# The first expert's rows turned by matmuls: known rows gathered early, the last two tiles put in with token-by-slot matrices

## The reference

```python
hp = hp + _mix_out(attn_p, bp * conv_p, ...)          # output projection
tok = concat([_rmsnorm(hp), _rmsnorm(hs)])            # 1032 tokens x 1024
g_sel = argmax(tok @ w_rg + b_rg)                     # one of 4 groups
le_sel = (tok @ w_re + b_re)[group g_sel]             # 8 logits
top_v, top_i = lax.top_k(le_sel, 2)
gates = softmax(top_v) * p_group[g_sel]
# for each expert e, over the rows that chose it:
hid = silu(xb @ w_gate[e]) * (xb @ w_up[e])           # 1024 -> 512
y = hid @ w_down[e]                                   # 512 -> 1024
# out = residual + gates[0] * y0 + gates[1] * y1, then a final norm
```

## Time and profile before

| | us |
|---|---|
| median of 3 runs | 1163.91 |
| lowest to highest run | 1163.84 to 1164.36 |
| the profiled execution's own time | 1163.65 |
| its span | 1161.8 |
| TensorE busy in the span | 1129.5 |
| VectorE busy | 826.4 |
| ScalarE busy | 640.8 |

### The profile page before, as it was taken

The page is one execution under the profiler, slowest core; times in us unless marked ns, Lnnn a source line. Parts: engine busy times, 40 slices in busy tenths (PEclk is TensorE's granted clock), DMA queues, the critical chain, the costliest instruction groups (busy, mean ns, idle before and its releaser), DMA issues.

```text
span 1161.8 us, 17492 instructions
## 1 busy us (share of the span) xinstructions
PE 1129.5 (97%) x7026; PEld 884.7 (76%) x7026; DVE 826.4 (71%) x1172; ACT 640.8 (55%) x796; POOL 106.3 (9%) x130
## 2 busy tenths in 40 slices
PE   7999999999999999999999999999999999999994
PEld 6999999999857768886677777777777777777761
DVE  5314434322387658887898898898898898889886
ACT  7221230211078732334577777777777777778744
POOL 1002110012000000000011100101100100112110
PEclk9999999999999999998999999999999999999998
DMA  8116474333050051114999999999999999999777
GB/s 257 55 44 194 126 240 160 119 109 110 5 179 21 26 221 73 74 73 163 372 400 399 384 391 382 388 399 381 382 391 385 381 393 383 383 388 376 308 266 292
DMA packets 77941, 292.54 MB, mean 252 GB/s; under 512 B 9689, under 2 KB 34393, under 8 KB 52962
## 3 DMA queue, kind: packets, MB, share of 16 engines
q1 hardware_dynamic: 66178, 259.78, 59.0%
q0 software_dynamic: 11680, 31.62, 8.3%
HBM read 270.09 MB, written 33.77 MB: 262 GB/s over the span
## 4 chain that ended last, share of the span: by engine, by line
PE 92%; DVE 4%; DMA 2%; ACT 1%; issue 1%; SPq 0%; DVEq 0%; POOLq 0%; ACTq 0%
PE psum L1190 10%; PE psum L1188 10%; PE psum L1189 10%; PE psum L854 8%; PE psum L856 8%; PE psum L855 8%; PE psum L1217 5%; PE psum L1219 5%; PE psum L1218 5%; PE psum L989 3%; PE psum L991 2%; PE psum L990 2%; PE psum L1177 2%; PE psum L939 2%; PE psum L955 1%; PE psum L933 1%
## 5 line engine op out<-in xcount | busy, mean ns | idle before, releaser
L854 PE MATMUL psum<-h_hi,w_hi 128*128 128x344 f32 (+2 forms) x576 | 185.8, 323 | 3.1 <-DVE h_lo L1684 3.0
L856 PE MATMUL psum<-h_hi,w_lo 128*128 128x344 f32 (+2 forms) x576 | 184.0, 319 | 0.0
L855 PE MATMUL psum<-h_lo,w_hi 128*128 128x344 f32 (+2 forms) x576 | 184.0, 319 | 0.0
L2115 DVE TENSOR_TENSOR w_down_lo<-w_down,w_down_hi 128x2048 fp32r<-128x2048 f32 x62 | 139.7, 2288 | 40.6 <-ACT w_down_hi L1507 40.6
L2115 DVE TENSOR_TENSOR w_gate_lo<-w_gate,w_gate_hi 128x2048 fp32r<-128x2048 f32 x64 | 144.2, 2288 | 20.7 <-ACT w_gate_hi L1507 19.4
L2115 DVE TENSOR_TENSOR w_up_lo<-w_up,w_up_hi 128x2048 fp32r<-128x2048 f32 x64 | 143.7, 2286 | 2.4
L1507 ACT CAST w_gate_hi<-w_gate 128x2048 fp32r<-128x2048 f32 x64 | 119.6, 1911 | 9.1 <-DMA w_gate<-in_w_gate 8.8
L1507 ACT CAST w_up_hi<-w_up 128x2048 fp32r<-128x2048 f32 x64 | 119.9, 1917 | 2.2 <-DMA w_up<-in_w_up 2.1
L1507 ACT CAST w_down_hi<-w_down 128x2048 fp32r<-128x2048 f32 x62 | 115.7, 1906 | 3.9 <-DMA w_down<-in_w_down 3.9
L854 PEld LDWEIGHTS psum<-h_hi,w_hi 128*128 128x128 f32 x576 | 108.2, 188 | 5.5 <-DVE h_lo L1684 3.9
L856 PEld LDWEIGHTS psum<-h_hi,w_lo 128*128 128x128 f32 x576 | 108.2, 188 | 0.0
(11 more groups left out here) (287 smaller groups left out, 1911.6 us busy)
## 6 DMA issues: line engine op xcount, KB each, us to landing
w_gate<-in_w_gate SPq DMA_DIRECT2D x64, 1024.0 KB, 16.2
w_up<-in_w_up SPq DMA_DIRECT2D x64, 1024.0 KB, 17.3
w_down<-in_w_down SPq DMA_DIRECT2D x64, 1024.0 KB, 15.5
w_raw<-in_w_in SPq DMA_DIRECT2D x24, 512.0 KB, 4.0
y_tile<-y_rows SPq DMA_DIRECT2D x16, 512.0 KB, 10.4
kv<-in_cache_k POOLq DMA_DIRECT2D x24, 256.0 KB, 4.6
kv<-in_cache_v POOLq DMA_DIRECT2D x24, 256.0 KB, 4.6
x_tile<-in_x_prompt SPq DMA_DIRECT2D x8, 512.0 KB, 5.5
```

The costliest lines, as they stand in the source:

```text
L854: mm(ps, wh[:, k, :], h_hi[:, k, cols], start=(k == 0), stop=False)
L855: mm(ps, wh[:, k, :], h_lo[:, k, cols], start=False, stop=False)
L856: ins = mm(ps, wl[:, k, :], h_hi[:, k, cols], start=False, stop=(k == KD - 1))
L2115: vec.tensor_tensor(dst[:, part, :], src[:, part, :], hi[:, part, :].bitcast(F32), ALU.subtract).then_inc(split, 1)
```

## The change

The table in HBM is laid out so that the seven tiles finished first come first (`token_row`: 776 rows, `KNOWN`), and the last two tiles last. After `place` of p = 6, which TensorE now does one step earlier, VectorE makes the first expert's indices from the table so far (`rows_known`), and GpSimd gathers those rows into a cleared buffer `xg_first`; slots whose tokens are in the last two tiles are still empty in that table, are dropped by the bounds check and stay zero.

TensorE puts these rows into PSUM with eight matmuls against the identity (`first_rows_fetched`), and adds the last two tiles straight from `h2` in SBUF: eight matmuls each of `h2` with a 0/1 matrix `chosen` of token by slot (`first_rows_chosen`). VectorE builds `chosen` from the rank in PSUM with `unchosen`, which moves tokens that did not choose the expert out of range (`choose_rows`).

The `keep_clock(3)`, `keep_clock(5)` and `keep_clock_narrow(12)` matmuls are gone. The first expert's products are written apart: for gate, then up, hi x hi and lo x hi (`first_upper`), then the count for further blocks, then both hi x lo series (`first_lower`). VectorE does `lower_rows` right behind the last tile's count, before the tables, and the splits of gate and up before `count_all`. `fetch_issued` is gone, so SyncE's loads are no longer held back by it; the second expert's down load waits for `xT_ready`, since its buffer is `xg_first`'s.

```diff
+KNOWN = NTOK - 2 * P
+def token_row(t):
+    return P * (t - 2) if t >= 2 else KNOWN + P * t
...
@@ SyncE
-            load_gate(first, 1, 1, (0,))
+            load_gate(first, 1, 1)
             store_h2(NT - 1)
-            sp.wait_ge(fetch_issued, 1)
-            load_gate(first, 1, 1, (1,))
+            load_down(first, 0, 0)
             load_up(first, 1, 1)
-            load_down(first, 0, 0)
+            store_residual(NT - 1)
+            sp.wait_ge(first.xT_ready, 2)
             load_down(first, 1, 1)
-            store_residual(NT - 1)
@@ TensorE
                     if n == 3:
                         route_pair(p - 1, 0)
                         route_pair(p - 1, 1)
+                        if p == NT - 1:
+                            place(p - 2)
...
-            keep_clock(3, bank(0), 512)
+            def first_rows_fetched():
+                pe.wait_ge(lg_used, NT)
+                pe.wait_ge(first.rows_in, 16)
+                for k in range(KD):
+                    mm(bank(4 + k // 4)[:, (k % 4) * SLOTS:(k % 4 + 1) * SLOTS], xg_first[:, k * P:(k + 1) * P],
+                       ident[0:SLOTS, 0:SLOTS], start=(k % 4 == 0), stop=True, skip_group_check=True)
+            def first_rows_chosen(p):
+                w = rows(turn[p])
+                pe.wait_ge(h2_ready, p + 1)
+                pe.wait_ge(chosen_ready, p - (NT - 2) + 1)
+                for k in range(KD):
+                    ins = mm(bank(4 + k // 4)[:, (k % 4) * SLOTS:(k % 4 + 1) * SLOTS],
+                             h2[p % 2][0:w, k * P:(k + 1) * P], chosen[p % 2][0:w, :], start=False, stop=True,
+                             skip_group_check=True)
+                    if p == NT - 1 and k % 4 == 3:
+                        ins.then_inc(first.xT_ready, 1)
+            first_rows_fetched()
+            first_rows_chosen(NT - 2)
             rank(NT - 1)
+            first_rows_chosen(NT - 1)
             place(NT - 1)
...
-            keep_clock(5, bank(0), 512)
-            keep_clock_narrow(12)
-            pe.wait_ge(routed, 1)
-            pe.wait_ge(first.rows_in, 16)
-            turn_rows(first)
+            first_upper(wg_hi, 0, first.gate_hi)
+            first_upper(wu_hi, 1, first.up_hi)
             count_all()
+            first_lower(wg_lo[0], 0, first.gate_split, first.gate_done)
+            first_lower(wu_lo[0], 1, first.up_split, first.up_done)
@@ ScalarE
+            act.wait_ge(h2_out[1], 16 * 4)
+            upper_rows(first, 0)
             act.wait_ge(gd_ready, 1)
             nc.scalar.activation(r_g, r_g, ACT.Exp)
             nc.scalar.activation(r_v, r_v, ACT.Exp).then_inc(gexp_ready, 1)
-            upper_rows(first, 0)
@@ VectorE
+            def choose_rows(p, e):
+                w = rows(turn[p])
+                step(vec.tensor_scalar(unchosen[p % 2][0:w, :], r_hot[p % 2][0:w, e:e + 1], DROP, -DROP,
+                                       ALU.mult, ALU.add))
+                if p == NT - 1:
+                    router_rows(p)
+                dve.wait_ge(ranked, p + 1)
+                vec.scalar_tensor_tensor(out=chosen[p % 2][0:w, :], in0=ramp[0:w, 0:SLOTS],
+                                         scalar=unchosen[p % 2][0:w, :],
+                                         in1=bank(6)[0:w, NE + e:NE + e + 1].broadcast_to([w, SLOTS]),
+                                         op0=ALU.add, op1=ALU.is_equal).then_inc(chosen_ready, 1)
...
+            rows_known(order[0])
             choose_first(NT - 2)
...
             recip_ffn(NT - 1)
+            choose_rows(NT - 2, order[0])
             slots_of(NT - 2)
             choose_first(NT - 1)
             choose_second(NT - 1)
-            router_rows(NT - 1)
+            choose_rows(NT - 1, order[0])
             slots_of(NT - 1)
+            count_tile(NT - 1)
...
+            lower_rows(first, 0)
             dve.wait_ge(hot_used, 2 * NT)
...
-            dve.wait_ge(fetch_issued, 1)
             lower_gate(first, 0, 0)
+            lower_up(first, 0, 0)
             count_all()
-            lower_rows(first, 0)
-            lower_up(first, 0, 0)
             finish_gates()
@@ GpSimd
+            pool.wait_ge(a_ready, NT - 1)
+            gp.memset(xg_first, 0.0).then_inc(rows_clear, 1)
+            pool.wait_ge(h2_out[0], 16 * 4)
+            pool.wait_ge(h2_out[1], 16 * 3)
+            pool.wait_ge(rows_clear, 1)
+            pool.wait_ge(routed, 1)
+            fetch(first, gi_s, xg_first, KNOWN)
             pool.wait_ge(h2_out[0], 16 * 5)
             pool.wait_ge(h2_out[1], 16 * 4)
-            pool.wait_ge(routed, 1)
-            fetch(first, gidx[:, order[0]:order[0] + 1])
-            gp.memset(stat[0:1, 82:83], 0.0).then_inc(fetch_issued, 1)
-            pool.wait_ge(y_cleared, 16 * NT)
+            pool.wait_ge(routed, 2)
```

More of the change, by code:

```diff
@@ L65, in constants @@
     c = np.arange(P)[None, :]
-    tok = 128 * np.arange(NT)[None, :] + p + 1
+    tok = np.array([token_row(t) for t in range(NT)])[None, :] + p + 1
     const = np.concatenate([
@@ L239, in program @@
         r_tab2 = rt_end("r_tab2", [NE])
+        chosen = [rt_end(f"chosen{s}", [SLOTS]) for s in range(2)]
+        unchosen = [rt_end(f"unchosen{s}", [1]) for s in range(2)]
         over = Pack(WEI + 3 * 16384, WEI + 4 * 16384)
@@ L382, in program @@
         all_sent = sem("all_sent")
-        fetch_issued = sem("fetch_issued")
+        rows_clear = sem("rows_clear")
         table_warm = sem("table_warm")
@@ L704, in store_h2 @@
                 sp.wait_ge(h2_ready, p + 1)
-                sp.dma_start(h2_d[P * t:P * t + rows(t), :], h2[p % 2][0:rows(t), :]).then_inc(h2_out[p % 2], 16)
+                sp.dma_start(h2_d[token_row(t):token_row(t) + rows(t), :], h2[p % 2][0:rows(t), :]).then_inc(h2_out[p % 2], 16)
             def store_residual(p):
@@ L1115, in place @@
                     mm(bank(7)[0:SLOTS, 0:NE], hot_slot[c][0:w, :], hot[p % 2][0:w, :],
-                       start=(p == 0 and c == 0), stop=(p == NT - 1 and c == 1)).then_inc(hot_used, 1)
+                       start=(p == 0 and c == 0), stop=True, skip_group_check=True).then_inc(hot_used, 1)
             square_sums(0)
@@ L1915, in count_tile, with rows_known @@
                 dve.wait_ge(summed, p + 1)
+            def rows_known(e):
+                tab = bank(7)[0:SLOTS, e:e + 1]
+                row, drop = r_tab[0:SLOTS, 0, 0:1], r_tab2[0:SLOTS, 0:1]
+                dve.wait_ge(hot_used, 2 * (NT - 2))
+                vec.tensor_scalar(drop, tab, 0.0, DROP, ALU.is_equal, ALU.mult)
+                step(vec.tensor_scalar(row, tab, float(NTOK), -float(NTOK), ALU.is_gt, ALU.mult))
+                step(vec.scalar_tensor_tensor(out=row, in0=tab, scalar=-1.0, in1=row, op0=ALU.add, op1=ALU.add))
+                step(vec.tensor_tensor(row, row, drop, ALU.add))
+                vec.tensor_copy(gi_s, row).then_inc(routed, 1)
+            def choose_rows(p, e):
[9 more added lines that the diff above has]
+                                         op0=ALU.add, op1=ALU.is_equal).then_inc(chosen_ready, 1)
             def slots_of(p):
@@ L1995, in token_rows, with lower_rows @@
                 follow(vec.scalar_tensor_tensor(out=dest, in0=tab, scalar=-1.0, in1=drop, op0=ALU.add, op1=ALU.add))
+            def lower_rows(f, n):
+                for half in range(2):
+                    dve.wait_ge(f.xT_hi_done, 2 * n + (half + 1))
+                    k = slice(4 * half, 4 * half + 4)
+                    vec.tensor_tensor(xT_lo[:, k, :], bank(4 + half)[:, 0:4 * SLOTS].rearrange("p (k t) -> p k t", k=4),
+                                      xT_hi[:, k, :].bitcast(F32), ALU.subtract).then_inc(f.xT_lo_done, 1)
+            lower_rows(first, 0)
             dve.wait_ge(hot_used, 2 * NT)
             token_rows(bank(7)[0:SLOTS, 0:NE], r_tab[0:SLOTS, 0, :], r_tab[0:SLOTS, 1, :], r_tab2[0:SLOTS], step)
-            dve.wait_ge(h2_out[0], 16 * 5)
-            dve.wait_ge(h2_out[1], 16 * 4)
             vec.tensor_copy(sidx[:, 0:NE], r_tab[0:SLOTS, 1, :])
@@ L2011, in count_all @@
             def count_all():
-                count_tile(NT - 1)
                 dve.wait_ge(counted, 1)
@@ L2098, in table_further @@
                 over_step(vec.tensor_copy(gidx[:, NE:NBLK], o_tab[0:SLOTS, 0, :]))
-            def lower_rows(f, n):
-                for half in range(2):
-                    dve.wait_ge(f.xT_hi_done, 2 * n + (half + 1))
-                    k = slice(4 * half, 4 * half + 4)
-                    vec.tensor_tensor(xT_lo[:, k, :], bank(4 + half)[:, 0:4 * SLOTS].rearrange("p (k t) -> p k t", k=4),
-                                      xT_hi[:, k, :].bitcast(F32), ALU.subtract).then_inc(f.xT_lo_done, 1)
             def lower_weight(dst, src, hi, chunks, ready, n, split, halves=(0, 1)):
```

53 lines of the change are left out of this document (32 added, 21 removed).

## The result

The changed kernel takes 1165.73 us (median of 20 runs, 1162.51 to 1168.43), the kernel before in the same rounds 1163.54 (20 runs, 1161.51 to 1164.73). The ratio is 1.0022, 95% interval 1.0016 to 1.0029: slower by about 2.2 us, where 1160.4 was forecast, in a range of 1159.2 to 1163.4. The profiled execution took 1167.01 us and had a mean granted clock of 0.984 (before: 0.992); it is slower than most of its runs, and its clock is lower than in most. Time and clock go together from run to run: the run of 1162.51 had 0.990, those of 1164.3 to 1164.7 had 0.987, those of 1166.5 and more 0.983 to 0.985.

A forecast was written before the change was run, and what follows sets the result against it. VectorE's queue from 534 up to the second expert's `xT_lo` was taken as the bound. Closed waits of 5.63 less 1.10, 0.40 and 0.6 gave 3.5 us gained: 1160.4 us, range 1159.2 to 1163.4.

The forecast's parts named there:

- The chain: VectorE's queue from 534 to `xT_lo` at 571.79 sets the second expert's gate product, whose start moves the end equally.
- The four waits, 5.63 us: VectorE's idle before 548.60, 552.05, 558.22 and 567.37 (0.23, 1.36, 1.57, 2.47 us) would all close.
- VectorE's additions, 1.10: Two `unchosen` at 0.24 and two `chosen` at 0.31 on VectorE cost 1.10 us.
- the moved `place`, 0.40: On TensorE, four `place` records at 0.10 ahead of tile position 7's last routing matmuls delay VectorE's logits 0.40 us.
- nothing is under 0.19: Floor for one added VectorE instruction, from a 32-column row, bounding the additions at 0.76 us or more.
- The new wait for the ranks, 0.6: VectorE, after the last `h`, waits 0.6 us for `ranked` behind the first two groups; the one new wait.
- A group, 0.12 a record, double at the low clock: Each new TensorE group, 16 records on 96 columns, takes 1.9 us, at twice the price in the low spell.
- The clock in the first stretch: First low spell stays, 542.0 to 545.4, at twice the price; the second, 548.8 to 552.2, is gone.
- one more spell: Rival: 545.4 to 548.8 is low too, or 548.8 to 552.2 stays low; gain 1.8 or 1.7, 1162.2 us; chance 0.22.
- both at once: Clause of the low-spell rival: both further stretches at low clock take the gain to nothing.
- price for the late casts, 1.8: If 548.8 to 552.2 stays low, the third group ends 552.4 and ScalarE's casts 553.0, 1.8 us late.
- The gathers: First issued near 533.5, landed by 541.5 at worst, needed at 542.8; second issued near 553.3, landing by 561.3.

The follow-up runs named there:

- second kernel: Changed kernel plus two 512-column matmuls nobody reads, one ahead of the `place` and one ahead of the `rank` before the first narrow group: 1159.73 us, ratio to before 0.9968.
- fifth kernel: Changed kernel plus fillers ahead of `rank` and `place` before the narrow groups, and three 512-column matmuls ahead of the second gate product: 1157.99 us, ratio to before 0.9956.
- Experiment 6: Changed kernel with the old `keep_clock(3)` put back ahead of the first narrow group: 1163.71 us, ratio to before 1.0004.
- experiment 2: Changed kernel plus two 512-column fillers nobody reads, ahead of the `rank` and the `place` before the narrow groups: 1159.73 us, ratio to before 0.9968.
- experiment 10: Changed kernel plus one 512-column filler, only ahead of the `place` before the narrow groups: 1165.94 us, ratio to before 1.0016.
- experiment 1: Changed kernel plus five 512-column matmuls nobody reads, ahead of the second expert's gate product: 1164.09 us, ratio to before 1.0005.
- 8: The fifth kernel plus a fourth narrow group, eight fp32 matmuls of 96 columns nobody reads, ahead of the last `rank`: 1159.98 us, ratio to before 0.9973.
- 11: The fifth kernel with the first expert's products in the old order on TensorE: 1161.44 us, ratio to before 0.9985.
- 12: The fifth kernel plus one more 512-column filler, ahead of the second expert's transposes: 1158.30 us, ratio to before 0.9957.

## Why the prediction was wrong

*The chain: right, with one gap.* VectorE's own queue sets the second gate product, and this the end. In the second kernel VectorE shows no idle time from the last h to `xT_lo`, and the product moves by 4.52; in the fifth the end moves with it. The gap: "what moves the start of the second expert's gate product moves the end by as much" took the clock behind that start as given. In the changed kernel the start moved by 1.24 and the end by 3.4.

*The four waits, 5.63 us: right.* All close with the clock at 1.00.

*VectorE's additions, 1.10, and the moved `place`, 0.40: too dear.* The last h comes 0.86 later than before where 1.19 was forecast, of which `place` is 0.24 (534.17 against 533.93), and 0.22 follow: 0.84 and 0.24. A `chosen` takes 0.31 as forecast, but the next instruction starts 0.23 behind its start; an `unchosen` takes 0.15, and the next starts 0.19 behind, where I took 0.24. The bound "nothing is under 0.19" was misread: in the kernel before, rows of one column take 0.15 (539.47). With both terms as measured and no new wait the sum is 5.63 - 0.84 - 0.24 = 4.55, and the second kernel's product moved by 4.52.

*The new wait for the ranks, 0.6: at 1.00 of the clock none; in the changed kernel 2.98, and 1.71 more for the casts.*

*A group, 0.12 a record, double at the low clock: right in both.* 1.83 and 3.49 us for 16 records, 0.114 and 0.218. The estimate by the Trainium skill ("TensorE: Matmul & The Clock Gate", section "LDWEIGHTS (loading the stationary operand)"), 1.7, was a little further off.

*The clock in the first stretch: this step failed.* I wrote: "Ahead of the first spell nothing changes, so I keep it, with twice the price; ahead of the second TensorE idled and now has the first two groups, so I take it as gone." The spell began about where it had (0.8 us earlier), but I took its length of 3.4 us as fixed. In the kernel before, six keep-clock records on 512 columns, one of the three removed series, ran from 541.52 to 545.88, and the clock came back in them, near 545.4. With the groups in their place it came back only at 558.2, during the first eight products on 512 columns: 17 us instead of 3.4. Experiment 6 shows that the clock comes back with the series put back, and experiments 2 and 10 what the long spell costs, some 6 us. The rival "one more spell" was the right mechanism, and its clause "both at once" was what happened. It was priced at no gain and gave 1.24 of loss at the second gate product: the wait for the ranks was 2.98 and not 2.3, and the one for `w_gate_hi`, which the rival took as closed, kept 0.92, since the first products ran at half rate too. Its price for the late casts, 1.8, was near the 1.71 measured.

*The second spell: a term that the sum did not have.* Its own walk has TensorE turn the rows near 563.5 and start the product at 569.0, so some 5 us of idle time; I counted that as slack and did not ask for the clock behind it. It cost 2.3. The Trainium skill, same page, section "Why this matters for your kernels", warns of idle gaps between bursts of matmuls. The changed kernel and experiment 1 agree for this gap: 4.91 of idle time and 0.51 behind it, 1.00 with the gap filled. I had set that warning beside the removed matmuls only. It does not cover the groups: TensorE was busy in 6.90 of 6.90 us from 541.9 to 548.8, at 0.50.

*The gathers: the first right, the second too short.* The first was never waited for; the known rows were in. For the second I took 8 us from issue to landing. In the fifth kernel it was issued at 552.87, and TensorE could turn its rows only at 564.20, 11.3 behind, after a wait of 1.48. It cost nothing there, as VectorE came later still.

*Left open.* What the clock goes by is not shown; only where it fell and came back, and what TensorE did there. Why the place filler alone held it in three runs of ten is not known. A single wide matmul in place of the two of experiment 2 was tried at their two places only. The tail behind the last expert's transposes took 64.0 to 65.9 us in the traces, which blurs spans by more than a microsecond. That, and the 1.2 us in the projection, were not looked into.

## What to carry to other kernels

When a change takes out matmuls that nobody reads, list every low spell of the granted clock and ask of each what stands ahead of its end, not only of its begin: the end may be the work of what is removed. Then walk the new schedule for TensorE's gaps too, as slack on TensorE is a price for what comes next. If the clock has to be held by filler, put it ahead of the fall (2 us of filler, 6 us won here), try it in several runs, and read the mean clock of each run beside its time, for one profile may show the rarer of two levels.

## What the hardware showed that I had not expected

- TensorE busy does not mean a full clock: it was 0.50 from 541.9 to 548.8 in the changed kernel with TensorE busy in all of it, nearly all on fp32 matmuls of 96 columns, and 1.00 in the same groups in experiments 2, 5, 6, 8, 10, 11 and 12. In all of these traces they kept the level that they started at.
- One program can run at either level: in experiment 10 three runs took about 1160 to 1162 us and seven 1165 to 1167.
- The second expert's gather takes GpSimd 0.99 us to issue before and 2.89 in the changed kernel (and in the fifth); no run tells why. The changed kernel's gathers for the second and third expert:

```profile
557.81 2.89 POOL L2314 DMA_INDIRECT x_rows<-h_rows,gidx  x1 [23.08 <-DVE gidx L2080]
569.61 2.14 POOL L2314 DMA_INDIRECT x_rows<-h_rows,gidx  x1 [8.91 <-PE psum L1211]
```
